# Gate and up of the first two feature tiles with the token tiles stationary, in a two-block network on one Trainium2 core

## What is computed

```python
def first_block(x, ...):
    for layer in range(DEPTH):               # DEPTH = 2
        h = rms_norm(x, attn_norm[layer])
        ...                                  # attention, x = x + mix @ w_out
        h = rms_norm(x, ffn_norm[layer])
        gate, up = jnp.split(h @ w_gate_up[layer], 2, axis=-1)
        x = x + (jax.nn.silu(gate) * up) @ w_down[layer]
    return rms_norm(x, final_norm)
```

## Time and profile before

| | us |
|---|---|
| median of three runs | 1015.75 |
| lowest, highest | 1013.6, 1016.22 |
| the profiled execution | 1019.5 |
| its span, first to last instruction | 1017.7 |
| TensorE busy with matmuls | 927.9 (91%) |
| VectorE busy | 656.7 (65%) |
| ScalarE busy | 493.5 (48%) |

### The profile page before, as it was taken

The page is one execution under the profiler, slowest core; times in us unless marked ns, Lnnn a source line. Parts: engine busy times, 40 slices in busy tenths (PEclk is TensorE's granted clock), DMA queues, the critical chain, the costliest instruction groups (busy, mean ns, idle before and its releaser), DMA issues. The chain is left out here.

```text
span 1017.7 us, 14878 instructions
## 1 busy us (share of the span) xinstructions
PE 927.9 (91%) x5660; PEld 789.1 (78%) x5660; DVE 656.7 (65%) x1223; ACT 493.5 (48%) x904; POOL 80.5 (8%) x87
## 2 busy tenths in 40 slices
PE   5997779899999999999899999998998789879887
PEld 3786437799999878866699999886897468768765
DVE  4776993555655457876645655546876957887464
ACT  5344562454545335476544544434544635445641
POOL 2000000000000000000000000003454000230010
PEclk9996878899999999999899999999998899999799
DMA  8464002366556556533546555665853025533101
GB/s 326 137 218 146 1 1 83 120 190 200 175 166 229 188 180 202 174 104 105 155 138 201 169 167 198 220 189 151 264 176 126 0 68 178 170 117 104 63 1 41
DMA packets 96790, 148.69 MB, mean 146 GB/s; under 512 B 6272, under 2 KB 59680, under 8 KB 96592
## 3 DMA queue, kind: packets, MB, share of 16 engines
q1 hardware_dynamic: 94512, 140.50, 43.3%
q10 hardware_dynamic: 1296, 4.83, 1.4%
q0 software_dynamic: 912, 2.41, 1.0%
HBM read 146.67 MB, written 1.05 MB: 145 GB/s over the span
## 5 line engine op out<-in xcount | busy, mean ns | idle before, releaser
L1009 DVE TENSOR_TENSOR w_lo<-w_raw,w_hi 128x1024 fp32r<-128x1024 f32 (+2 forms) x269 | 319.9, 1211 | 141.9 <-ACT w_hi L617 137.8
L617 ACT ACTIVATE w_hi<-w_raw 128x1024 fp32r<-128x1024 f32 (+2 forms) x269 | 274.4, 1042 | 156.8 <-DMA w_raw<-in_w_gate_up 64.7
L1705 PE MATMUL ps<-hT_hi,w_lo 128*128 128x256 f32 x768 | 219.5, 286 | 3.4 <-DVE w_lo L1009 1.9
L1706 PE MATMUL ps<-hT_hi,w_hi 128*128 128x256 f32 x768 | 219.0, 285 | 0.0
L1707 PE MATMUL ps<-hT_lo,w_hi 128*128 128x256 f32 x768 | 218.9, 285 | 0.0
L1705 PE MATMUL ps<-w_hi,hT_lo 128*128 128x512 f32 (+3 forms) x416 | 162.4, 390 | 10.9 <-DVE w_lo L1009 4.5
L1707 PE MATMUL ps<-w_lo,hT_hi 128*128 128x512 f32 (+3 forms) x416 | 158.7, 382 | 0.0
L1706 PE MATMUL ps<-w_hi,hT_hi 128*128 128x512 f32 (+3 forms) x416 | 158.6, 381 | 0.0
L1705 PEld LDWEIGHTS ps<-hT_hi,w_lo 128*128 128x128 f32 x768 | 149.2, 194 | 4.5 <-ACT z L686 2.1
L1706 PEld LDWEIGHTS ps<-hT_hi,w_hi 128*128 128x128 f32 x768 | 149.2, 194 | 0.0
L1707 PEld LDWEIGHTS ps<-hT_lo,w_hi 128*128 128x128 f32 x768 | 149.2, 194 | 0.0
(11 more groups left out here) (234 smaller groups left out, 1200.7 us busy)
## 6 DMA issues: line engine op xcount, KB each, us to landing
w_raw<-in_w_gate_up SPq DMA_DIRECT2D x176, 256.0 KB, 4.3
w_raw<-in_w_down SPq DMA_DIRECT2D x44, 512.0 KB, 4.2
w_raw<-in_w_in_e SPq DMA_DIRECT2D x38, 512.0 KB, 5.2
w_raw<-in_w_qkv_o SPq DMA_DIRECT2D x24, 512.0 KB, 4.3
w_raw<-in_w_in_o SPq DMA_DIRECT2D x20, 512.0 KB, 3.6
w_raw<-in_w_out_e SPq DMA_DIRECT2D x16, 512.0 KB, 4.3
w_raw<-in_w_out_o SPq DMA_DIRECT2D x16, 512.0 KB, 3.5
w_raw<-in_w_in_e SPq DMA_DIRECT2D x8, 268.0 KB, 2.7
```

The source lines that it names most:

```text
L617: n.activation(w_hi[:, u % RING, 0:size], w_raw[:, u % RING, 0:size], ACT.Copy).then_inc(hi_ready, 1)
L1009: v.tensor_tensor(w_lo[:, u % RING, 0:size], w_raw[:, u % RING, 0:size], w_hi[:, u % RING, 0:size].bitcast(F32), ALU.subtract).then_inc(lo ...
L1705: m.matmul(o, lhs[1], rhs[0], start=start, stop=False)
L1706: m.matmul(o, lhs[0], rhs[0], start=False, stop=False)
```

## The change

On TensorE chunk 0 of gate and up is done in another layout. For each token tile t the tile (`hT_hi`, `hT_lo`) is stationary and 512 weight columns (256 gate, 256 up) move: 24 matmuls of width 512 for each token tile, into bank `g % 4` with g = 22 x layer + t. `norm_tile` of token tile 1 no longer stands ahead of `ffn`, but ahead of the fourth unit of token tile 0. Silu and the multiplication work on 128 tokens x 256 features, as many elements as before. Their two products lie with tokens on partitions, so four transposes behind feature tile 2 (a new fill `hidden0` or `hidden1`) turn them; ScalarE and VectorE split them from PSUM, 128 x 512 at once, ahead of and behind the split of chunk 3. Chunks 1 to 10 are as before. The first multiplication of chunk 1 waits for the transposes, since it writes the buffer that they read.

```diff
-for _name, _n in [("norm0", 4), ("prep0", 11), ("cmp_p", 1), ("attn0", 24), ("norm1", 4), ("norm2", 4)]:
+for _name, _n in [("norm0", 4), ("prep0", 11), ("cmp_p", 1), ("attn0", 24), ("norm1", 4), ("hidden0", 1),
+                  ("norm2", 4)]:
...
-for _name, _n in [("norm3", 4), ("norm5", 4), ("prep2", 7), ("attn2", 16), ("norm6", 4), ("lora", 2)]:
+for _name, _n in [("norm3", 4), ("hidden1", 1), ("norm5", 4), ("prep2", 7), ("attn2", 16), ("norm6", 4), ("lora", 2)]:
...
         def ffn(layer):
-            for j in range(FT):
+            split(LAST[f"gu{layer}", 0] + AHEAD)
+            for t in range(NT):
+                g = layer * FT + t
+                if t:
+                    act.wait_ge(units_used, LAST[f"gu{layer}", 0])
+                else:
+                    act.wait_ge(even_up, layer * FT // 2 + 1)
+                if g >= 2:
+                    act.wait_ge(hid32_ready, g - 1)
+                n.activation(silu_g[:, t, :], ps[:, g % 4, 0:T], ACT.Silu).then_inc(silu_ready, 1)
+            f = FILL[f"hidden{layer}", 0]
+            for j in range(2, FT):
+                if j == 4:
+                    act.wait_ge(t_filled, f + 1)
+                    n.activation(hid_hi[:, 0:2, :].rearrange("p j t -> p (j t)"), ps[:, TB + f % 2, :], ACT.Copy)\
+                     .then_inc(sem("first_hid_hi"), 1)
                 g = layer * FT + j
...
         def ffn(layer):
+            f = FILL[f"hidden{layer}", 0]
             for j in range(FT):
                 g = layer * FT + j
                 if j % 2 == 0:
                     split(LAST[f"gu{layer}", j // 2] + AHEAD)
+                if j == 2:
+                    dve.wait_ge(t_filled, f + 1)
+                if j == 4:
+                    dve.wait_ge(sem("first_hid_hi"), layer + 1)
+                    v.tensor_tensor(hid_lo[:, 0:2, :].rearrange("p j t -> p (j t)"), ps[:, TB + f % 2, :],
+                                    hid_hi[:, 0:2, :].rearrange("p j t -> p (j t)").bitcast(F32), ALU.subtract)\
+                     .then_inc(t_drained[f % 2], 1)
...
+                if j < 2:
+                    continue
...
         def ffn(layer):
-            for c in range(FT // 2):
+            for t in range(NT):
+                g = layer * FT + t
+                for u in range(FIRST[f"gu{layer}", 0], LAST[f"gu{layer}", 0]):
+                    if t == 0 and u == LAST[f"gu{layer}", 0] - 1:
+                        norm_tile(1 + 2 * layer, 1)
+                    pe.wait_ge(lo_ready, u + 1)
+                    wh, wl = halves(u)
+                    for i in range(2):
+                        kk = UNITS[u][2] + i
+                        tile_ready(1 + 2 * layer, t, kk)
+                        l = tuple(b[:, kk, t * P:(t + 1) * P] for b in (hT_hi, hT_lo))
+                        ins = product(ps[:, g % 4, :], l, (wh[:, i, :], wl[:, i, :]), kk == 0, kk == KT - 1)
+                    if t:
+                        ins.then_inc(units_used, 1)
+                if t == 0:
+                    ins.then_inc(even_up, 1)
+            f = FILL[f"hidden{layer}", 0]
+            for c in range(1, FT // 2):
...
+                    if j == 2:
+                        pe.wait_ge(hid32_ready, layer * FT + 2)
+                        open_fill(f)
+                        for b in range(2):
+                            for t in range(NT):
+                                ins = m.transpose(ps[:, TB + f % 2, b * T + t * P:b * T + t * P + P],
+                                                  hid32[:, t, b * P:(b + 1) * P], ident)
+                        ins.then_inc(t_filled, 1)
...
         project_out("w_out_e", "attn0", 1)
-        norm_tile(1, 1)
         ffn(0)
...
         project_out("w_out_o", "attn1", 3)
-        norm_tile(3, 1)
         ffn(1)
```

More of the change, by code:

```diff
@@ L1117, in ffn @@
                  .then_inc(hid32_ready, 1)
-                dve.wait_ge(hid_hi_ready, g + 1)
+                if j < 2:
+                    continue
+                dve.wait_ge(hid_hi_ready, g + 1 - 2 * (layer + 1))
                 v.tensor_tensor(hid_lo[:, j, :], hid32[:, g % 2, :], hid_hi[:, j, :].bitcast(F32), ALU.subtract)\
@@ L1819, in ffn @@
                                 kk = UNITS[u][2] + k
-                                if c == j == gate == 0:
-                                    tile_ready(1 + 2 * layer, 1, kk)
                                 ins = product(ps[:, g % 4, T * gate:T * gate + T],
@@ L1833, in down @@
                 pe.wait_ge(lo_ready, u + 1)
-                pe.wait_ge(hid_ready, layer * FT + j + 1)
+                if j < 2:
+                    drained(f)
+                else:
+                    pe.wait_ge(hid_ready, layer * (FT - 2) + j - 1)
                 wh, wl = halves(u)
```

## The result

| | before | changed |
|---|---|---|
| median, us | 1015.99 (4 runs, 1013.6 to 1016.62) | 1001.94 (4 runs, 998.59 to 1005.45) |
| ratio to before, 95% interval | | 0.9867 (0.9839 to 0.9895) |
| profiled execution, us | 1019.5 | 998.59 |
| a second set of runs, median us | 1016.56 (16 runs, 1011.43 to 1023.29) | 1000.48 (4 runs, 997.71 to 1006.61) |
| ratio there, 95% interval | | 0.9839 (0.9802 to 0.9876) |

The change saves 14 us by the first set (10.7 to 16.4 by its interval) and 16 by the second (12.6 to 20.1). Single runs of one kernel spread by up to 12 us here, so the stages are compared in the traces. The page of the changed kernel: its head line, which answers to the earlier trace rows, and its row for TensorE.

A forecast was written before the change was run, and what follows sets the result against it. It took TensorE, busy in 91% of the span, as the bound, so only its own stream or holes counted. Layer gains 6.0 + 6.5 - 0.4 = 12.1 us, from 1015.75, gave 1003.6 us; range 1000.5 to 1007.5.

The forecast's parts named there:

- TensorE's holes and the early start: Both seams: instead of idling 3.75 us, TensorE starts gate and up on token tile 0 at 183.8 and 499.6.
- 48 matmuls at 0.227: Chunk 0 of gate and up: 48 matmuls of width 512, 0.227 us each, take 10.9 us per layer.
- rivals 2 and 3: At the seams matmuls run slow: about 15 per layer (1009.7 us, chance 0.06) or all 48 (1023.3 us, chance 0.03).
- Rival 2: Clock falls part way at the seams: about 15 matmuls per layer stay slow, 6.1 us, giving 1009.7; chance 0.06.
- The insertion doesn't wait: Token tile 1's transposes reach TensorE at about 188.1 and 503.9, with `hA` complete at 187.98 and 503.77.
- The insertion of eight transposes: Token tile 1's eight transposes amid the 48 matmuls of chunk 0 cost 1.25 us per layer.
- Four more transposes: The four new transposes behind feature tile 2 cost 0.8 us per layer, between 0.5 and 1.25, without waiting.
- Weights of chunk 1: VectorE's `w_lo` splits end almost exactly when TensorE wants chunk 1; 0.2 us charged per layer, ends 0 and 0.7.
- Rival 1: Ahead of chunk 1 `w_lo` arrives one split (1.16 us) later in each layer, giving 1005.9 us; chance 0.10.
- The flip of the fills: Second attention: `prep1` fills 6 and 7 change engine, so probability transposes wait for VectorE; 0.4 us lost, ends 0 and 1.0.
- Rival 4: The fill flip disturbs the second attention by more than one wait, giving 1005.2 us; chance 0.06.
- The base: Starting time for the gain: the runs' median 1015.75 us, 3.75 below the profiled execution of 1019.5.

The follow-up runs named there:

- e2_norm_first: The changed kernel with the transposes of token tile 1 put back ahead of gate and up in both layers; median 1014.31 us.
- e4_earlier: The changed kernel with the transposes of token tile 1 one unit (6 matmuls) earlier in token tile 0; 997.17 us in a single run.
- e6_vector_late: The changed kernel with one more VectorE instruction, its result unused, ahead of the splits of chunk 1 in each layer; 1006.74 us in a single run.

## Why the prediction was right, step by step

The forecast was 12.1 us less, 1003.6, and 1001.94 was measured. That lies within the range, 1000.5 to 1007.5, but just below the sum's own lower end of 1002.2. The likeliest case came in, and none of the rivals. By step:

- **TensorE's holes and the early start.** Right. The first matmul of gate and up starts 0.50 us (layer 0 by its entry, 176.25 in the trace) and 0.59 us (485.71) behind the last of the projection; 0.58 and 0.59 had been put in.
- **48 matmuls at 0.227.** Right (187.94 is the last, and between neighbours it is 0.22 to 0.23). The first distance behind each turn is 0.31, so the 48 take 11.0 us and not 10.9. Clock 1.00, no slow stretch: rivals 2 and 3 fell. The eight transposes in the stream did nothing to it. Rival 2 would have cost less than it said: it took 15 wide matmuls to be slow, as many as there were narrow ones, and behind the same hole e2_norm_first has 9 and 8.
- **The insertion doesn't wait.** Right, by less than the prediction had it and partly by luck. Its own terms, 183.8 + 4.1, give 187.9 and not the 188.1 that it wrote (503.7 and not 503.9 in layer 1), just ahead of the end of VectorE's scaling and not behind it. Measured, the transposes start at 180.45 and `hA` is complete at 179.10 + 1.41 = 180.51. There is no wait, since the first four need only the first half of `hA`, which the prediction left out.
- **The insertion of eight transposes: too dear.** I took 1.25. It is 181.25 - 180.22 - 0.23 = 0.80 and 0.09 more at the next matmul. The row that I took it from (181.20 to 182.68) held a wait: the start at 181.61 is 0.41 behind its neighbour and not 0.23, and the eight take 1.07 us to the next matmul, as in e4_earlier, where they wait for VectorE's scaling. In layer 1 it is 490.68 - 489.65 - 0.23 = 0.80 again. Mis-sized by 0.4 in each layer.
- **Four more transposes: too dear.** Taken 0.8, measured 193.79 to 194.27, 0.36 over the usual 0.12, and 0.08 at the next matmul: 0.44, below my lower bound of 0.5. The turn to another shape costs about 0.1 (the 0.08), not 0.3. Mis-sized by 0.4 in each layer.
- **Weights of chunk 1.** Taken 0.2 each, measured 0 in layer 0 and 0.2 in layer 1 (0.08 ahead of chunk 1 and 0.11 at its second matmul). The chain from the first transpose to the last split takes 187.78 - 180.45 = 7.33 us and 497.61 - 489.89 = 7.72, against the 7.6 to 8.5 that were taken. "The cover ends almost exactly" was right: e6_vector_late shows 0.3 us of room and none. Rival 1 fell.
- **The flip of the fills.** Right in its place and size: 0.4 taken, 0.34 and 0.36 measured. It turned two waits of 0.39 and 0.57 into one of 1.48. Rival 4 fell.
- **The sum.** 12.1 against 13.7 by the seams. Of the 1.6 between them the two kinds of transposes give 1.4 (0.36 each, in each layer), the weights 0.3 (by the seams, which end at chunk 1's first matmul), the start and the flip 0.1 together, and the dearer 48 matmuls take 0.2 back. All the large terms err to the same side, and the mechanism is the one forecast.
- **The base.** I held the profiled execution at 1019.5 to be 3.75 us above the median and moved both by the same gain. Right, but the trace of after came 7.5 us shorter than the gain in it. The range had 1 or 2 us for the spread of a median; single runs of one program spread by 9 to 12 us.

## What to carry to other kernels

Where a stage must wait for the last token tile's norm, begin it with the tokens stationary: the tiles that are ready can be multiplied while the norm of the others runs, and the price is a handful of transposes, if later work wants features on partitions. Place the transposes by comparing two times, the producer's end and the count of matmuls ahead; one unit wrong cost 1.1 to 1.4 us on either side here. And compare two profiled executions by stage, from one common event to the next, with the granted clock of each stage beside it: their totals here were 20.9 us apart, of which 13.4 were the change and 7.5 the clock of two stretches ahead of it.

## What the runs showed of the hardware that I had not expected

- Up to layer 0's seam ten traces of code that differs at most by 24 small matmuls reach the same point at 174.1 to 182.0 us. One stretch of that code takes 7.2 us at a mean granted clock of 0.90 and 10.9 at 0.50, another 22.9 at 1.00 and 26.8 at 0.84, while 58 us in which VectorE is the busy engine take the same at 0.76 and 0.84.
- The clock can fall after a hole has ended: in layer 1 of e2_norm_first, behind 3.75 us without work, TensorE had been working again for 1.4 us, eight transposes and a matmul, when the matmuls became slow; in layer 0 of the same trace the transposes were slow already (1.62 us to the next matmul).
- Eight float32 transposes of 128 x 128 inserted in a dense stream cost 0.80 us, 0.10 each, and 0.09 more behind the next matmul; that is less than the 0.134 each that the row of eight before, with a wait in it, suggests.
